# Router logits from unscaled rows, a shorter rank chain, and one quarter of down weights asked for later

## The reference, cut to what matters

```
def hier_moe(h, w_rg, w_re, w_gate, w_up, w_down):      # h = rmsnorm(x, g_moe_norm)
    pg = softmax(xf @ w_rg)                             # 4 groups
    g_top = argmax(pg);  pg_top = max(pg)
    fl = (xf @ w_re) of group g_top                     # 4 experts in it
    top_p, top_i = top_k(softmax(fl), 2)
    wts = top_p / sum(top_p) * pg_top
    act = silu(xf @ w_gate[e]) * (xf @ w_up[e]) * wts   # width 512, 16 experts
    return sum over the two experts of act @ w_down[e]
x = x + hier_moe(...);  y = rmsnorm(x, g_final)
```

## Time and profile before

| what | us |
|---|---|
| median of three runs | 1712.69 |
| the profiled execution's own time | 1712.43 |
| its span, first to last instruction | 1710.6 |
| busy: TensorE matmul, VectorE, ScalarE, GpSimd | 1476.1, 361.1, 289.6, 77.9 |
| first gather of rows issued, landed | 1116.59, 1125.09 |
| first expert product starts | 1128.10 |

### The profile page before, as it was taken

The page is one execution under the profiler, slowest core; times in us unless marked ns, Lnnn a source line. Parts: engine busy times, 40 slices in busy tenths (PEclk is TensorE's granted clock), DMA queues, the critical chain, the costliest instruction groups (busy, mean ns, idle before and its releaser), DMA issues. The chain is left out here.

```text
span 1710.6 us, 18748 instructions
## 1 busy us (share of the span) xinstructions
PE 1476.1 (86%) x7256; PEld 756.7 (44%) x7256; DVE 361.1 (21%) x864; ACT 289.6 (17%) x619; POOL 77.9 (5%) x109
## 2 busy tenths in 40 slices
PE   7999999999999978877899999669789867898780
PEld 3444445555555656643454565433233223333230
DVE  2101010000322165465210203611001000010015
ACT  3000000012322134355100103100000000000001
POOL 0000000001100000000000000001010100011000
PEclk9999999999999889979899999879899998999995
DMA  8375224422430077400934124879999999899965
GB/s 345 140 313 186 99 95 148 161 87 99 148 148 13 7 221 240 140 10 1 356 102 148 50 99 183 312 268 395 402 355 387 412 388 399 355 401 414 406 271 188
DMA packets 113805, 380.22 MB, mean 222 GB/s; under 512 B 17459, under 2 KB 55387, under 8 KB 83047
## 3 DMA queue, kind: packets, MB, share of 16 engines
q1 hardware_dynamic: 108050, 343.27, 53.3%
q0 software_dynamic: 5552, 27.89, 4.8%
q10 hardware_dynamic: 144, 8.26, 1.1%
HBM read 390.41 MB, written 26.49 MB: 244 GB/s over the span
## 5 line engine op out<-in xcount | busy, mean ns | idle before, releaser
L2262 PE MATMUL bank<-W,hT_e 128*64 128x512 f32 x576 | 274.3, 629 | 64.6 <-DMA w_u<-in_w_exp_up 63.7
L2263 PE MATMUL bank<-w_u,hT_e 128*64 128x512 f32 x576 | 274.2, 629 | 0.0
L2262 PEld LDWEIGHTS bank<-W,hT_e 128*64 128x64 f32 x576 | 80.5, 144 | 251.0 <-issue 158.8
L2279 PE MATMUL bank<-W,actT 128*64 128x512 f32 x576 | 138.1, 635 | 9.0 <-ACT actT L2290 9.0
L490 PE MATMUL bank<-raw,hT 128*128 128x512 f32 (+1 forms) x320 | 132.9, 577 | 0.6 <-PEq L243 0.6
L728 PE MATMUL bank<-subT,w 128*128 128x504 f32 (+1 forms) x320 | 132.7, 545 | 0.0
L490 PE MATMUL bank<-w_in,hT 128*128 128x512 f32 (+2 forms) x320 | 123.7, 547 | 0.0
L1633 PE MATMUL bank<-W,mixT 128*128 128x512 f32 x256 | 112.6, 600 | 1.6 <-DVE mixT L1868 1.6
L490 PEld LDWEIGHTS bank<-raw,hT 128*128 128x128 f32 x320 | 62.0, 195 | 68.4 <-issue 68.1
L490 PEld LDWEIGHTS bank<-w_in,hT 128*128 128x128 f32 x320 | 60.4, 190 | 61.0 <-issue 61.0
L2308 DVE SCALAR_TENSOR_TENSOR act_w<-bank,row_w,gate 64x512 f32<-64x512 f32 x18 | 13.6, 757 | 335.6 <-ACT gate L2288 335.6
(11 more groups left out here) (378 smaller groups left out, 1544.1 us busy)
## 6 DMA issues: line engine op xcount, KB each, us to landing
W<-in_w_exp_down SPq DMA_DIRECT2D x76, 1024.0 KB, 23.5
W<-in_w_exp_gate SPq DMA_DIRECT2D x72, 1024.0 KB
w_u<-in_w_exp_up SPq DMA_DIRECT2D x72, 1024.0 KB
raw<-in_w_in SPq DMA_DIRECT2D x3, 4096.0 KB
W<-in_w_out SPq DMA_DIRECT2D x3, 4096.0 KB, 13.4
w_in<-in_w_in SPq DMA_DIRECT2D x2, 4096.0 KB, 14.6
k_in<-in_cache_sel_k SPq DMA_DIRECT2D x64, 128.0 KB, 2.1
v_in<-in_cache_sel_v SPq DMA_DIRECT2D x64, 128.0 KB, 3.5
```

What stands on the lines that cost most here:

```text
L2262: pe.matmul(bank[4 + u][0:NS, :], hT[:, u, c, :], w_g[:, c, :], start=(c == 0), stop=(c == KC - 1))
L2263: mm = pe.matmul(bank[4 + u][UP, :], hT[:, u, c, :], w_u[:, c, :], start=(c == 0), stop=(c == KC - 1))
L2279: mm = pe.matmul(bank[2 * u + n // 2][lane, :], actT[:, q, :], w_d[:, u, q, 512 * n:512 * n + 512], start=(q == 0), stop=(q == 3))
```

## The change

In the first block TensorE transposes the rows of `x` themselves (`turn_x`), as soon as they are added. ScalarE and VectorE copy the results to `mixT` without a gain, two of four pieces each (`keep_moe`). Tiles 0 and 1 are turned before `w_o_block` of tile 2, tile 2 after the logits of the other two, and the logits are made in two parts, of 256 and of 64 columns. VectorE multiplies the router weights by the gain once, before the memory attention. The tile `ms`, which holds each row's factor, is kept for the router block, and so moves ahead of `W` among the buffers; there the 20 logits are multiplied by it. In the router block the eight instructions that serve only `experts` and `pairs` are moved behind `planes`. The fourth quarter of `down_loads(1, 1)` is asked for in the third block, after GpSimd has issued the first gather.

```
+        ms = sb(top, "ms_late", [P, 2, TILES])            # ahead of W; before: in the block's own scope
...
+                    def turn_x(r):                        # TensorE
+                        pe.wait_ge(added, 12 + 4 * r + 4)
+                        for j in range(4):
+                            k = 2 * r + j // 2
+                            if k:
+                                pe.wait_ge(moe_kept[j % 2], k)
+                            for c in range(4):
+                                mm = pe.transpose(bank[T_BANKS[MOE][j % 2]][:, c * P:c * P + ROWS[r]],
+                                                  x[0:ROWS[r], r, 4 * j + c:D:KC], ident[0:ROWS[r], 0:ROWS[r]])
+                            mm.then_inc(turned, 1)
...
-                    turn(MOE, 0)
+                    turn_x(0)
+                    turn_x(1)
                     pe.wait_ge(s_placed_a, 1)
                     pe.wait_ge(s_placed_d, 1)
                     for n in range(4):
                         w_o_block(2, n)
-                    turn(MOE, 1)
...
-                    logits(0)
-                    turn(MOE, 2)
-                    logits(1)
-                    logits(2)
+                    pe.wait_ge(wr_padded, 2)
+                    for v in range(2):
+                        pe.wait_ge(moe_kept[v], 4)
+                    logits(0, 2 * P)
+                    turn_x(2)
+                    for v in range(2):
+                        pe.wait_ge(moe_kept[v], 6)
+                    logits(2 * P, TOK)
...
+                    def keep_moe(r):                      # ScalarE: j in (0, 2); VectorE: j in (1, 3)
+                        for j in (0, 2):
+                            act.wait_ge(turned, 24 + 4 * r + j + 1)
+                            act.copy(mixT[...], bank[T_BANKS[MOE][0]]...).then_inc(moe_kept[0], 1)
...
                     square_moe(1, 3)                      # ScalarE
+                    keep_moe(0)
+                    keep_moe(1)
                     root(7, ms[:, 1, 1:2])
                     for n in range(4):
                         square_moe(2, n)
+                    keep_moe(2)
                     root(8, ms[0:NS, 1, 2:3])
...
+                    dve.memset(ms[:, :, :], 0.0)          # VectorE, first block
...
+                    dve.wait_ge(wr_loaded, 32)            # before the copies L1925
+                    dve.tensor_tensor(w_r[:, :, 0:20], w_r[:, :, 0:20], gain_moe[...], ALU.mult).then_inc(wr_padded, 1)
...
                     add_moe(1, 3)
-                    drain(MOE, 0)
+                    keep_moe(0)
+                    keep_moe(1)
                     stats(1, 1)
                     normalise(1, 1)
                     for n in range(4):
                         add_moe(2, n)
+                    keep_moe(2)
                     stats(1, 2)
                     normalise(1, 2)
-                    drain(MOE, 1)
-                    drain(MOE, 2)
...
-                    for dst, src, loaded in down_loads(1, 1):          # SyncE, router block
+                    for dst, src, loaded in down_loads(1, 1)[0:3]:
...
-                    L(dve.tensor_copy(lg[:, :, :], bank[0][:, 0:60]...))
+                    L(dve.tensor_tensor(lg[:, :, :], bank[0][:, 0:60]..., wide(ms[:, 1, :], 20), ALU.mult))
...
+                    # total, owner, owner_f, halves, experts, total, pairs: from between pick
+                    # and past (L2120 to L2130) to behind planes (L2139), ahead of the wait for the table
...
+                    sp.wait_ge(first_asked, 1)                         # SyncE, third block, before L2187
+                    for dst, src, loaded in down_loads(1, 1)[3:4]:
+                        sp.dma_start(dst, src).then_inc(loaded, 16)
...
                     gather(0, 0)                                       # GpSimd
+                    pool.sem_inc(first_asked, 1)
```

More of the change, by code:

```diff
@@ L1532, in trunk @@
             ms_part = sb(scope, "ms_part", [P, 2, TILES, 4])
-            ms = sb(scope, "ms_late", [P, 2, TILES])
+            moe_kept = [sem(f"late_moe_kept{v}") for v in range(2)]
             stat = sb(scope, "m_stat", [P, 3, 2, MH])
@@ L1828, in keep_o @@
                         act.copy(o_mT[:, :, r * P:r * P + P], bank[2 + r].rearrange("p (h r) -> p h r", h=MH)).then_inc(o_kept, 1)
+                    def keep_moe(r):
+                        for j in (0, 2):
+                            act.wait_ge(turned, 24 + 4 * r + j + 1)
+                            act.copy(mixT[:, 4 * j:4 * j + 4, r * P:r * P + ROWS[r]],
+                                     bank[T_BANKS[MOE][0]].rearrange("p (c r) -> p c r", c=4)[:, :, 0:ROWS[r]]).then_inc(moe_kept[0], 1)
                     def square_moe(r, n):
@@ L1871, in drain, with keep_moe @@
                                               ALU.mult).then_inc(drained, 1)
+                    def keep_moe(r):
+                        for j in (1, 3):
+                            dve.wait_ge(turned, 24 + 4 * r + j + 1)
+                            dve.tensor_copy(mixT[:, 4 * j:4 * j + 4, r * P:r * P + ROWS[r]],
+                                            bank[T_BANKS[MOE][1]].rearrange("p (c r) -> p c r", c=4)[:, :, 0:ROWS[r]]).then_inc(moe_kept[1], 1)
                     def add(to, r, n):
@@ L1921, in _ @@
                     drain(MEM, 2)
+                    dve.wait_ge(wr_loaded, 32)
+                    dve.tensor_tensor(w_r[:, :, 0:20], w_r[:, :, 0:20], gain_moe[:, :].unsqueeze(2).to_broadcast([P, KC, 20]), ALU.mult).then_inc(wr_padded, 1)
                     for h in range(MH):
@@ L2118, in _ @@
                                                 sel[:, r, :, :], ALU.mult)
[L2119 to L2127, removed]
+                    L(dve.tensor_tensor(pick[:, 1], start_at[:, :].unsqueeze(1).to_broadcast([P, PAIRS, NE]), selj, ALU.mult))
+                    L(dve.reduce_sum(rank[:, 0:2, :], pick[:, :, :, :], AX))
                     L(dve.tensor_tensor(past[:, :, :], rank[:, 0, :].unsqueeze(2).to_broadcast([P, PAIRS, 4]),
                                         cst("tile_over")[:, 1:5].unsqueeze(1).to_broadcast([P, PAIRS, 4]), ALU.is_ge))
-                    dve.tensor_copy(pairs[:, :], total[:, 1:2])
                     L(dve.reduce_sum(rank[:, 2, :], past[:, :, :], AX))
@@ L2140, in _ @@
                     ins.then_inc(planes_ready, 1)
+                    dve.tensor_tensor(total[:, 0:1], start_at[0:1, NE - 1:NE], tiles[0:1, NE - 1:NE], ALU.add)
+                    L(dve.tensor_tensor(owner[:, :, :], start_at[0:1, :].unsqueeze(1).to_broadcast([1, TURNS_MAX + 2, NE]),
+                                        cst("turn_no")[0:1, :].unsqueeze(2).to_broadcast([1, TURNS_MAX + 2, NE]), ALU.is_le))
+                    dve.reduce_sum(owner_f[:, :], owner[:, :, :], AX)
+                    L(dve.tensor_scalar(halves[:, :], cst("pair_no")[0:1, :], total[:, 0:1], None, ALU.is_lt))
+                    dve.tensor_scalar(experts[:, :], owner_f[:, :], -1.0, None, ALU.add)
+                    L(dve.reduce_sum(total[:, 1:2], halves[:, :], AX))
+                    dve.tensor_copy(pairs[:, :], total[:, 1:2])
                     dve.wait_ge(table_made, 1)
@@ L2167, in trunk @@
             gathered = [sem(f"e_gathered{v}") for v in range(2)]
-            gf_loaded = sem("f_gf_loaded")
+            gf_loaded, first_asked = sem("f_gf_loaded"), sem("e_first_asked")
             y_loaded = [sem(f"f_y_loaded{r}") for r in range(TILES)]
```

11 lines of the change are left out of this document (4 added, 7 removed).

## The result

The changed kernel was timed against the kernel before three times, the second and third time on two more chips:

| comparison | changed, median (runs) | before, median (runs) | ratio, 95% interval |
|---|---|---|---|
| the one forecast | 1716.94 (6) | 1709.24 (6) | 1.0032 (1.0018 to 1.0047) |
| second | 1714.82 (12) | 1712.63 (35) | 1.0004 (0.9991 to 1.0018) |
| third | 1716.21 (12) | 1712.16 (23) | 1.0021 (1.0005 to 1.0038) |

What follows compares the result with a forecast made beforehand. The first gather's landing, starting the DMA-bound stretch, was taken to bound the kernel. Terms -0.8 (turning x early), -1.4 (rank chain) and -0.1 (gather) gave -2.3 us, from 1712.43 to 1710.1, range 1705 to 1716.

Steps and rivals of the forecast that it cites:

- What bounds the kernel: Long DMA-bound stretch from 1134.5 us: the kernel's end moves one for one with the first gather's landing.
- the 9.44 us from landing to ask: Between the first gather's landing and turn 1's gate quarter request: 9.44 us, so the long stretch starts earlier with the landing.
- Part 1: First block, turning x early: the block ends at 1094.6 against 1095.38, gain 0.8 us (bounds 2.5 gain, 1.0 loss).
- Part 2: Gain on `w_r` in a 10.73 us VectorE gap: cost nothing; logits' multiply and cleared `ms`: 0 to 0.1 us together.
- Part 3: Rank chain in the router block: 1.4 us earlier (bounds 0.9 and 1.5), moved eight instructions hidden behind TensorE's table.
- Part 4: Weight traffic and first gather: issued at 1114.4, taking 8.4 us within the stream, landing at 1122.8 against 1125.09.
- Theory A: From the experiments: the first gather can't land before weights in front are through; the end follows the ask one for one.
- gather behind the backlog: Rival at the first gather: engines finish queued weights first, landing 7.1 us after the stream, +1.0 to +3.6 us; chance 0.17.
- one packet of weights at each engine: Round-robin DMA queues: a gather in a full stream waits for only this much, not for the whole backlog.
- The held quarter: Turn 1's fourth down quarter, 1 MB, asked for behind the first gather: main weight stream ends 2.6 us sooner.
- Its second side: SyncE's wait for the held quarter before asking for the gate quarter: cost 0, with 5 us of cover.
- theory B: From the experiments: the long stretch keeps only part of a shift; the remaining difference goes with the granted clock.

Runs made afterwards that it cites:

- p0_same: The kernel before, unchanged, timed against itself; ratio 0.9992 (0.9977 to 1.0007).
- e5_ms: The kernel before with only the tile `ms` moved ahead of `W`; ratio 1.0002 (0.9985 to 1.0018).
- e1_rank: The kernel before with only the rank chain's new order, eight instructions moved behind `planes`; ratio 1.0031 (1.0010 to 1.0051), repeated at 1.0014.
- e2_rows: The kernel before with logits from unscaled rows alone (first-block edits, `ms` ahead of `W`, factor on logits), old rank chain, four quarters; ratio 1.0027.
- e4_no_quarter: The changed kernel with all four down quarters of turn 1 asked for in the router block again; ratio 1.0039 (1.0018 to 1.0061).
- e6_all_behind: The changed kernel with all four down quarters of turn 1 asked for only after the first gather's landing; ratio to before 0.9999.
- e7_late: The kernel before with two GpSimd memsets ahead of the first gather; ratio 1.0009 (0.9993 to 1.0025).
- e10_before_free: The kernel before, turn 1's down quarters behind the first gather's landing, gate and up quarters asked for ahead of the wait for them; ratio 0.9995.
- e9_free_ask: The changed kernel, turn 1's down quarters behind the first gather's landing, gate and up loop ahead of the wait for them; ratios to before 0.9991, 0.9989.
- e11_late15: The kernel before with eight GpSimd memsets ahead of the first gather; ratio 1.0074 (1.0056 to 1.0092).
- e1b: The same edit as e1_rank, the kernel before with only the rank chain's new order, measured again; ratio 1.0014 (0.9999 to 1.0028).
- e3: The kernel before with only the fourth down quarter of turn 1 held until after the first gather's issue; ratio 1.0025 (1.0008 to 1.0042).

## Why the prediction was wrong

| | issue | landing after it | ask | ratio |
|---|---|---|---|---|
| before | +42.9 | 8.5 | +60.8 | |
| p0_same, as before | +43.0 | 7.2 | +60.1 | 0.9992 |
| e5_ms, opening as before | +43.1 | 5.6 | +57.6 | 1.0002 |
| e1_rank, twice | +41.6, +41.6 | 10.0, 7.7 | +60.8, +57.9 | 1.0031, 1.0014 |
| e2_rows | +43.0 | 9.1 | +61.2 | 1.0027 |
| changed, three traces | +41.6, +41.6, +41.5 | 11.5, 11.0, 10.7 | +61.5, +61.2, +61.1 | 1.0032, 1.0004, 1.0021 |
| e4_no_quarter | +41.6 | 12.1 | +62.0 | 1.0039 |
| e6_all_behind | +41.6 | 5.6 | +62.8 | 0.9999 |
| e7_late | +46.8 | 5.6 | +61.1 | 1.0009 |
| e10_before_free | +43.0 | 5.6 | +57.6 | 0.9995 |
| e9_free_ask, twice | +41.6, +41.5 | 5.6, 5.5 | +56.9, +56.9 | 0.9991, 0.9989 |
| e11_late15 | +57.9 | 5.8 | +73.6 | 1.0074 |

**What bounds the kernel: right in the main.** The end follows the time at which the gate quarters are asked for (e11, and over all 16 comparisons 0.8 us per us of the first ask, a slope worked out from ask and ratio). The last of the four gate quarters tells it somewhat better than the first (correlation with the ratio 0.87 for 0.81, and without e11 0.75 for 0.59), and e6 is why. But the 9.44 us from landing to ask are no constant: 8.4, 8.6 and 8.8 us in the changed kernel, 9.95 in p0. In the changed kernel's profiled execution the granted clock over that stretch was 0.65, for 0.57, so of 1.7 us at the landing 0.6 arrived at the ask.

**Part 1: the mechanism right, the sum wrong.** `w_o_block` of tile 2 started 6.3 us after the first transpose instead of the 6.4 forecast, the relay's rounds were 1.4 us, and the store of tile 2 set the block's end. The lane sums of the router began 0.9 us earlier (+21.7 for +22.6). But that gain was lost again. The sums themselves took 1.47 us (L2062), where before they took 0.84:

```profile
1096.31 0.84 PE L2030 MATMUL bank<-const,part 128*128 128x20 f32 x6 [0.93 <-DVE part L2066]
```

TensorE now waits 2.55 us for VectorE before them and runs them at the clock's lower level, 1.2 GHz (granted 0.50, for 1.00 before). And from VectorE's last instruction to GpSimd's first 1.33 us passed instead of 0.93. That is so in all eight traces with the rows part, and 0.92 or 0.93 in the seven without it and without memsets; the reason stays open. e2_rows shows the net: 0.

**Part 2: right.** The gain's multiply (0.48 us) stands in the gap, 10.30 us of which are left, and from the first query copy to the first transpose 73.8 us pass in every trace, with it and without.

**Part 3: right to 0.1 us**, 1.44 us from `pick` to the table, the moved instructions done by 1109.92 while TensorE works until 1111.24. It is the only gain that reached the issue: 1.3 us instead of 2.2. Behind the weights it is lost; with the weights out of the way it arrives at the landing (+47.2 and +47.1 in e9, for +48.5 in e10), and 0.7 us of it at the ask.

**Part 4: the step that failed.** I took the median of the gathers, 8.4 us, for the first one. It took 11.5, 11.0 and 10.7 us in three traces, and the landing moved from +51.4 to +53.1, where 2.3 us earlier was forecast. The reason is the weights: kept away until the first gather has landed, they leave it 5.5 or 5.6 us from an issue at the same time (e6, e9 twice), and 5.55 us in the kernel before (e10). I had the numbers: the rows part makes the stream start later (3.5 us by SyncE's request, relative to the opening), and the gather is issued earlier into it. From the gather's issue to the ask SyncE's queue still moved 2.1 to 2.4 MB in the changed kernel, 1 MB of it the held quarter, and 0.55 MB in before. I had also read before's stream as ended at about 1118, though by the earlier trace rows SyncE waited for its last quarter until 1117.31 + 5.94 = 1123.25.

Where no weights are in its way a gather takes 5.5 to 5.8 us (e6, e7, e9 twice, e10, e11); with 0.37 MB left it took 5.6 in e5, with 0.48 MB 7.2 in p0. SyncE's wait for the last down quarter tells how long the stream ran: until 1123.25, +49.6, in before; in the other two with the same opening

```profile
1113.28 4.55 SPq L2189 DMA_DIRECT2D W<-in_w_exp_down  x4
```
```profile
1114.24 2.08 SPq L2189 DMA_DIRECT2D W<-in_w_exp_down  x4
```

until 1117.83, +48.2, in p0 and 1116.32, +45.9, in e5, where it was hardly a wait (1.97 us in e7, with the engines idle). The landings are +51.4, +50.1 and +48.7. So with before's order of requests the first gather lands at the later of its issue + 5.6 and this wait's end + 1.8 or 1.9 (1.8 in e1, e1b and e2, too), and before's profiled execution was one with a long stream: its 8.50 us were not a property of the gather.

This is no rule for the changed kernel. There the wait ended at +53.6, +53.6 and +55.0 and the landings were ahead of it, at +53.1, +52.6 and +52.3; in e4, too, by 2.7 us. Theory A's first half, that the gather can't land before the weights in front of it are through, doesn't hold as it stands. Nor is the stream's end a given: with no gather beside it, in e7 and e11, the wait ended at +45.8 and +46.1; beside a gather it ended later in four traces of five, at up to +49.9 (e1). The two run at the same time, and which holds up the other isn't shown; why executions of the same code differ by 3 us in this stays open. In before it was the slowest part of each: a transfer signals its landing 16 times; the last quarter's signals lie between 1117.61 and 1120.65 but for the last, at 1122.92, and the gather's between 1121.56 and 1123.11 but for the last, at 1125.09.

The rival "gather behind the backlog" named this cause and its point of decision (10.7 us from the issue), and gave it 0.17. Its argument against, "the longest of 19 is 10.6", rested on the other gathers; why those, in a full stream, take less than the first of the changed kernel no run shows. But the rival's mechanism, an engine that first finishes what is queued, isn't shown: a gather ends together with the stream, and not 7.1 us after it.

The Trainium skill's round-robin between queues (DMA: Bandwidth & Descriptors) doesn't contradict this, since the landing is of the slowest engine; but "one packet of weights at each engine" as the price, as I read it, is refuted by 11.5 against 5.6 us. The same page says that DMA engines 7 and 15 are usually slower; whether these are the ones that end late no row here tells.

**The held quarter** is worth less than 1 us (the ask of e3 is 0.4 us earlier than before's and 0.4 later than p0's, that of e4 0.5 to 0.9 later than the change's), where 2.6 us of stream were forecast: it runs beside the gather and not behind it. Its second side, SyncE's wait, was free in the changed kernel (1126.73 for an ask at 1134.55), but in e6 it took all of the gain at the first ask.

**The rest of the difference.** From before's family (+57.6 to +60.8, mean of three 59.5) to the changed kernel (mean 61.3) the ask moves by 1.8 us; the three comparisons say 3.1 (1.7 to 4.6). What is left is of the size by which single runs differ, and there theory B holds. Between runs of one program, 34 of before on one chip, the time goes with the mean granted clock (correlation -0.75, 4.5 us per 0.01), and they spread from 1702.73 to 1718.15. Most of a lower clock is hidden behind the stream, as in the turns of the stretch 1495 to 1545, first before, then changed:

```profile
1495.00:1545.00 50.00, 48.07 (x242) 19.04 (x239) 5.78 (x9) 4.61 (x8) 6.75 (x10) 1.00 1.01 404
```
```profile
1495.00:1545.00 50.00, 48.09 (x214) 18.34 (x212) 5.42 (x8) 4.21 (x7) 6.74 (x10) 0.86 1.01 401
```

At 0.86 of the clock the same 48 us of busy time hold 28 matmul records fewer, of identical code (some may be missing from the trace), but the weights run at a share of 1.01 in both. It isn't hidden where no weights are left to move. The two profiled executions ask at 1134.53 and 1134.55 and start their last down product within 0.3 us of each other:

```profile
1660.73 7.09 PE L2279 MATMUL bank<-W,actT 128*64 128x512 f32 x32 [0.54 <-ACT actT L2290]
```
```profile
1660.48 8.78 PE L2315 MATMUL bank<-W,actT 128*64 128x512 f32 x32 [0.54 <-ACT actT L2326]
```

At a granted clock of 0.81 for 1.00 it took 1.7 us longer, nearly all of the 1.8 us by which the two spans differ. That is no mark of the change: in p0 it took 8.64 us, and 7.09 in both other traces of the changed kernel. Whether the changed kernel meets a low clock more often by more than chance (mean clock 0.9185, 0.9216 and 0.9226 in its three comparisons, 0.9247 and 0.9228 for before in the last two) stays open, and with it some 1 us of the 3.

## What to carry to other kernels

Before shortening the chain that issues a transfer, look at what else the DMA engines have in front of them at that time: here 1.3 us of earlier issue brought no earlier landing, and keeping 4 MB of weights that nobody needed yet out of the way of a 0.5 MB gather was worth 4.5 us at the ask. When a request is moved behind another, check every wait on the same queue that stands for its landing, and put the asks that have become urgent ahead of it. Don't take a duration from one profiled execution where it depends on a race between two streams; the same opening gave 8.5, 7.2 and 5.6 us.

## What the runs showed of the hardware

A 1 MB transfer issued 0.39 us after the gather (at 1115.05 against 1114.66) doesn't keep it out of the gather's way: e3's gather took 8.0 us, inside the 5.6 to 8.5 us of the three traces of before's opening without the hold. Two SyncE edits that keep all four transfers away until the gather has landed gave 5.6 us (e10). The end of the same twelve 1 MB transfers, asked for within 1 us of the same times of the opening, varied from +45.9 at most (e5) to +49.6 (before), although both moved 424 GB/s from +30 to +40. A gather of 64 rows takes 5.5 to 5.8 us with the engines free (six traces) and 10.7 to 11.5 us with 2.1 to 2.4 MB of weights still to move (three traces).
